# Copying strided operands for the value products, two more weight buffers from a dead table, and expert rows of 8 KB

## The reference

```
first_block, two layers:   h += 0.5 * swiglu(rmsnorm(h))
                           h += mixer(rmsnorm(h))        layer 0: ab_mixer, layer 1: c_mixer
                           h += 0.5 * swiglu(rmsnorm(h))
                           h += sigmoid(rmsnorm(h) @ Wg) * (p @ Wp)
second_block:              recurrence, pooling and attention branches, gated, merged into h
                           h += expert_choice_ffn(rms_norm(h))
                           out = rms_norm(h)

ab_mixer:  qa, ka, va, qb, kb, vb = split(xn @ w_in)
           banded attention on (qa, ka, va); on (qb, kb, vb) three groups of heads
           with dilations 1, 4 and 16 (tokens of one residue class attend each other)
expert_choice_ffn:
           aff = softmax(h @ router)                     16 experts
           vals, idx = top_k(aff.T, 64)                  each expert takes 64 tokens
           xg  = h[idx]
           y   = (silu(xg @ w_gate) * (xg @ w_up)) @ w_down * vals
           out[idx] += y
```

## Time and profile before

| | |
|---|---|
| median of 3 runs | 3620.35 us (3615.5 to 3622.46) |
| the profiled execution | 3626.29 us, span 3624.9 us |
| TensorE, weight loads busy | 3329.7 us (92%), 2544.3 us (70%) |
| VectorE, ScalarE, GpSimd busy | 44%, 30%, 9% |
| value products of ab_mixer | about 509 to 577 us |
| experts, from the first gate product | about 3104 to 3625 us |
| DMA packets | 96660, 445.89 MB |

### The profile page before, as it was taken

How to read it: one execution, slowest core, us unless ns; L and a number is a source line. 1 busy time by engine, 2 the same in 40 slices (tenths; PEclk the granted TensorE clock), 3 DMA queues, 4 the chain that set the end, 5 groups by cost and what they waited for, 6 DMA issues and landing times.

```text
span 3624.9 us, 52383 instructions
## 1 busy us (share of the span) xinstructions
PE 3329.7 (92%) x22912; PEld 2544.3 (70%) x22912; DVE 1606.8 (44%) x2207; ACT 1086.9 (30%) x1684; POOL 320.7 (9%) x374
## 2 busy tenths in 40 slices
PE   8999999999999999999999999668768998978876
PEld 6888787888887888886788877457656886423323
DVE  4443546544336443327544337854475444101102
ACT  4222215432224222226422233444324324000001
POOL 1000111100000000001100002131141002000001
PEclk9999999999999999999999999889988999999998
DMA  3223320122223222332122223000020223699996
GB/s 132 95 89 98 124 82 13 47 93 93 91 94 106 99 93 88 110 117 82 59 97 101 84 91 106 29 32 5 4 78 18 88 102 124 264 409 409 409 410 255
DMA packets 96660, 445.89 MB, mean 123 GB/s; under 512 B 8496, under 2 KB 9648, under 8 KB 78768
## 3 DMA queue, kind: packets, MB, share of 16 engines
q1 hardware_dynamic: 96432, 442.53, 33.5%
HBM read 440.40 MB, written 2.10 MB: 122 GB/s over the span
## 4 chain that ended last, share of the span: by engine, by line
PE 81%; DMA 8%; DVE 7%; ACT 2%; issue 2%; POOL 0%; SPq 0%; DVEq 0%; POOLq 0%; ACTq 0%
PE bank L165 21%; PE bank L166 21%; PE bank L167 21%; PE bank L2182 4%; DMA xe<-in_exp_up 3%; PE bank L1584 3%; PE bank L769 2%; DMA xe<-in_exp_gate 2%; PE bank L736 2%; PE bank L1576 2%; PE bank L752 2%; DMA xe<-in_exp_down 2%; PE bank L2258 1%; PE bank L651 1%; DVE w_lo L471 1%
## 5 line engine op out<-in xcount | busy, mean ns | idle before, releaser
L471 DVE TENSOR_TENSOR w_lo<-slot,w_hi 128x2048 fp32r<-128x2048 f32 (+4 forms) x243 | 489.3, 2014 | 344.5 <-ACT w_hi L462 343.2
L165 PE MATMUL bank<-xa,w_hi 128*128 128x512 f32 x1368 | 546.0, 399 | 22.1 <-DVE xa L514 10.2
L166 PE MATMUL bank<-xa,w_hi 128*128 128x512 f32 x1368 | 534.0, 390 | 0.0
L167 PE MATMUL bank<-xa,w_lo 128*128 128x512 f32 x1368 | 534.0, 390 | 0.0
L462 ACT ACTIVATE w_hi<-slot 128x2048 fp32r<-128x2048 f32 (+4 forms) x243 | 405.8, 1670 | 384.9 <-PE bank L167 383.8
L165 PE MATMUL bank<-xb,w_hi 128*128 128x512 f32 x832 | 326.6, 393 | 9.0 <-DVE w_lo L471 9.0
L166 PE MATMUL bank<-xb,w_hi 128*128 128x512 f32 x832 | 324.7, 390 | 0.0
L167 PE MATMUL bank<-xb,w_lo 128*128 128x512 f32 x832 | 324.7, 390 | 0.0
L165 PEld LDWEIGHTS bank<-xa,w_hi 128*128 128x128 f32 x1368 | 257.8, 188 | 83.9 <-issue 11.1
L166 PEld LDWEIGHTS bank<-xa,w_hi 128*128 128x128 f32 x1368 | 258.0, 189 | 58.9 <-issue 6.5
L167 PEld LDWEIGHTS bank<-xa,w_lo 128*128 128x128 f32 x1368 | 257.8, 188 | 54.1
(11 more groups left out here) (410 smaller groups left out, 5193.1 us busy)
## 6 DMA issues: line engine op xcount, KB each, us to landing
slot<-in_w_gu SPq DMA_DIRECT2D x87, 1024.0 KB, 4.9
slot<-in_exp_gate SPq DMA_DIRECT2D x48, 1024.0 KB, 13.5
slot<-in_exp_up SPq DMA_DIRECT2D x48, 1024.0 KB, 14.1
slot<-in_exp_down SPq DMA_DIRECT2D x48, 1024.0 KB, 14.2
slot<-in_w_dn SPq DMA_DIRECT2D x64, 704.0 KB, 4.0
slot<-in_w_gate SPq DMA_DIRECT2D x24, 768.0 KB, 4.2
xe<-in_exp_gate SPq DMA_DIRECT2D x16, 1024.0 KB, 14.1
xe<-in_exp_up SPq DMA_DIRECT2D x16, 1024.0 KB, 14.1
```

The source lines that it names most:

```text
L165: e.matmul(out, w[0], x[0], start=(j == 0), stop=False)
L166: e.matmul(out, w[0], x[1], start=False, stop=False)
L167: return e.matmul(out, w[1], x[0], start=False, stop=(j == n - 1))
L471: dve.e.tensor_tensor(lo, slot(k, b), hi.bitcast(F32), ALU.subtract).then_inc(L.up("w_lo", b))
```

## The change

It has three parts. The values of groups 2 and 3 read copies `xc` of `xa`, in which the tokens of a class lie side by side. ScalarE copies the rounded parts (`act_classes`), GpSimd the rests (`pool_classes`), both after the last rotation; the copies lie over the buffers of the rotation and over `sq`. The eight expert blocks that a product needs are laid out on the host so that a partition's 2048 floats are one row of 8 KB; which numbers go to which partition stays the same. And the ring gets two buffers more, over the table `G`, from expert block 24 on, once the last product with `G` is done.

```diff
 def expert_block(w, e, j):
-    return w[e, j * 256:(j + 1) * 256, :].rearrange("(k p) c -> p k c", p=P)
+    return w[e, j]
...
+    sq_area = a.copy()
     k.sq, k.sqsum = [a.buf(512, "sq") for _ in range(2)], a.buf(512, "sqsum")
...
-    inner = a.copy()
+    inner, b = a.copy(), a.copy()
...
-    m.rT = a.buf(8, "rT")
+    m.rT = b.buf(8, "rT")
+    m.xc = [b.pair("xc") for _ in range(KT - 1)] + [sq_area.pair("xc")]
...
+    late = a.copy()
     m.G = a.buf(4096, "G", F32R).rearrange("p (i s) -> p i s", i=4)
...
+    k.slots += [late.buf(SLOT, "slot") for _ in range(2)]
...
-                                      4: ("h", "n10", 7), 5: ("h", "n10", 7), 6: ("turned_xe", 7), 7: ("turned_xe", 7)}
+                                      4: ("h", "n10", 7), 5: ("h", "n10", 7), 6: ("turned_xe", 7), 7: ("turned_xe", 7),
+                                      8: ("dispatched", 1, 7), 9: ("dispatched", 1, 7)}
...
+        if b == k.first["exp"] + 24:
+            slots = [8, 9] + slots
...
-def pe_values(k, st, g, b, width, x, sel):
+def pe_values(k, st, g, b, width, x, sel, ready=()):
...
         for j in range(KT):
+            for name in ready:
+                pe.wait_ge(*L.at(name, st, j))
             last = three(e, bank[:, 0:width], each(lambda p: sel(p, i), x[j]), at(w, j), j, KT)
...
+def act_classes(k):
+    act, e, L, m = k.act, k.act.e, k.led, k.ab
+    act.wait_ge(*L.at("roped", "ab", 19))
+    for j in range(KT):
+        e.activation(f4(m.xc[j][0]), cls(k.xa[j][0].bitcast(F32)), ACT.Copy).then_inc(L.up("class_hi", "ab", j))
+
+
+def pool_classes(k):
+    pool, e, L, m = k.pool, k.pool.e, k.led, k.ab
+    pool.wait_ge(*L.at("roped", "ab", 19))
+    for j in range(KT):
+        e.tensor_copy(f4(m.xc[j][1]), cls(k.xa[j][1].bitcast(F32))).then_inc(L.up("class_lo", "ab", j))
...
-        pe_values(k, "ab", g, b["ab_v"] + g, 256, k.xa, AB_SEL[g])
+        pe_values(k, "ab", g, b["ab_v"] + g, 256, *((k.xa, tok) if g < 2 else (m.xc, tok, ("class_hi", "class_lo"))))
...
         act_weight(k, b["ab_v"] + g + 1)
+        if g == 0:
+            act_classes(k)
...
+    pool_classes(k)
     pool_attention(k, "ab", m.att, ab_units(k))
...
     for name in ("exp_gate", "exp_up", "exp_down"):
-        a[name] = f[f"{name}_2"][0]
+        w = f[f"{name}_2"][0].reshape(16, 4, 2, P, 1024)
+        a[name] = np.ascontiguousarray(w.transpose(0, 1, 3, 2, 4)).reshape(16, 4, P, 2048)
```

More of the change, by code:

```diff
@@ L910, in ab_units @@
     return units
-def by_class(x, i):
-    return cls(x)[:, i, :]
-AB_SEL = [tok, tok, by_class, by_class]
+def act_classes(k):
[8 more added lines that the diff above has]
+        e.tensor_copy(f4(m.xc[j][1]), cls(k.xa[j][1].bitcast(F32))).then_inc(L.up("class_lo", "ab", j))
 def sp_ab(k):
```

## The result

| | median us | range of the runs | profiled execution, span |
|---|---|---|---|
| before | 3621.40 | 3615.50 to 3630.30 (4) | 3626.29, 3624.9 |
| changed | 3582.19 | 3577.32 to 3595.42 (4) | 3583.27, 3582.0 |
| changed, compared again on another chip | 3583.18 | 3578.27 to 3595.74 (6) | 3595.74, 3594.4 |

The ratio to before is 0.9895, with a 95% interval of 0.9862 to 0.9929; the second comparison gives 0.9884 (0.9861 to 0.9908). By the medians the change makes the kernel 39 us faster (26 to 50 by the interval). The forecast was 3587 in a range of 3579 to 3594.

A forecast was written before the change was run, and what follows sets the result against it. TensorE was taken to bound the long part, expert-weight transfers the experts' stage. Savings of 21.8 + 3.4 + 8.2 = 33.4 us from the median 3620.35 gave 3587 us, range 3579 to 3594.

The forecast's parts named there:

- What bounds each stage: Whole kernel: TensorE sets the pace in the values and the tail, expert-weight transfers from 3170.64 us to nearly the end.
- Part 1, the class copies: Attention values, groups 2 and 3: eight banks at 2.88 instead of 5.60 us save 21.8 us; copies cost nothing.
- the chain behind ScalarE's queue: After ScalarE's copies: emptying group 0's banks, then splitting the third value block; a split start up to about 527.5 is free.
- Part 2, two buffers: Experts, ahead of pair 1: block 24 is issued earlier, removing the dry stretch; 3.4 us saved, between 0 and about 4.
- Part 3, rows of 8 KB: Expert blocks 16 to 175: 0.051 us less on each of 160 blocks, 8.2 us saved (1.9 to 13.6).
- full help: Experts, sign to look for: steps of two blocks at 4.96 us if long rows help fully; 5.03 was forecast.
- the short rate of 8 KB rows holds: Experts, rival: 13.6 us instead of 8.2, and 1.7 more if the tail's slow clock goes; 3580 us, chance 0.15.
- they hardly help: Experts, rival: bytes set the ceiling, so long rows gain only 1.9 us; 3593 us, chance 0.2.
- The last 16 blocks: Experts' tail after block 175: no gain counted, because TensorE is the limit from there.
- the slower one: Experts, rival: full queues of 8 KB rows run at 348 GB/s, 3.01 us a block; 3677 us, chance 0.03.
- The copies were not late: Value group 2, rival: slow class-step copies make TensorE wait, 4.4 us lost at 3.5 us a GpSimd copy; 3591, chance 0.07.
- the slow clock: Tail, part at a granted clock of 0.50: losing or keeping it is worth 1.7 us either way.

The follow-up runs named there:

- more copies: Changed kernel with each class copy made three times on ScalarE and twice on GpSimd, each waiting for the one before; ratio 0.9908 to the kernel before.
- queries by class: Changed kernel with the rotation writing the dilated groups' queries in class order, so that score-product loads are contiguous; ratio 0.9888 to the kernel before.

## Why the prediction was right

- **What bounds each stage: right.** TensorE in the values, transfers in the experts, TensorE in the tail, though there the transfers end at nearly the same time.
- **Part 1, the class copies: right, 0.5 us small.** Forecast 21.8 us, measured 44.8 - 22.5 = 22.3. A contiguous load out of `xc` takes 188 ns, a little less than one out of `xa` in groups 0 and 1 (192). The copies cost nothing on the path, as argued: 1.06 us each on ScalarE, between my 0.7 and 1.4, and 10.8 us for all on GpSimd, within 9 to 14. The run with more copies shows what it costs when the cover is gone, and that the chain behind ScalarE's queue is the one that I named.
- **Part 2, two buffers: right.** Forecast 3.4 us, measured 3.3 alone, in D. The time of that kernel can't show it.
- **Part 3, rows of 8 KB: right in kind, small in size.** Forecast 0.051 us on a block and 8.2 us, measured 0.067 to 0.07 (D with the rows alone, and 2.56 to 2.49) and so 10.7 to 11.2 us for 160 blocks. Steps follow at 4.98 us, nearer to the 4.96 that I named for full help than to my 5.03. A cost by row, half of which goes, was right. The mis-sized term is that cost: I took 0.067 us for the 256 rows of a 4 KB block, as the difference between 409 and 420 GB/s. The three sizes give 0.146 for 256 rows (387 to 409 GB/s, 2.710 to 2.564 us), so half is 0.073. The 420 of a short window was no rate free of the rows' cost: by the line through the three sizes a block without it would take about 2.42 us, or 434 GB/s (an estimate). Short windows can lie above the long run with rows of 8 KB too: 427 GB/s between 3106 and 3112 us in the changed kernel. The rival that the short rate of 8 KB rows holds (13.6 us) was about as near as my forecast; the one that they hardly help (1.9 us) was far off.
- **The last 16 blocks: nearly right.** I took nothing for them. In the kernels with rows of 4 KB and the copies or the buffers alone, whose tails run at full clock, the last step does wait for DMA, by 0.7 us, and from the last up step to the end it is 77.0 us. With rows of 8 KB at full clock it is 76.0 (rows alone) and 76.1 (queries by class). So these blocks are worth about 0.9 us at full clock. In the profile of before the last step doesn't wait; there the half-clock stretch makes TensorE's last product 1.7 us longer (15.57 us up to the combination, against 13.88 with the rows alone), which covers the 0.7.
- **Sum.** 22.3 + 3.3 + 11.2 = 36.8 us by the stages, 33.4 forecast, and 39 by the medians (26 to 50 by the interval).
- **Rivals.** The time alone can't choose: the interval takes in all cases but the slower one, and 3582 is nearer to the 3580 of the rival with short rates than to my 3587. The stages choose. The copies were not late. Long rows brought 10.7 to 11.2 us and not 1.9. They were not 13.6 either, and the slow clock did not leave the tail of the profile. The slower case would need 388 GB/s and got 420. The Trainium skill ("DMA: Bandwidth & Descriptors", Why small descriptors are slow) gives a packet about 3 cycles beside its beats of 32 bytes, which makes an estimate of 1.1% for 8 KB rows. The runs show 2.6% (2.564 to 2.497 us at 409 and 420 GB/s), so these cycles are not the whole cost of a row in this kernel, and the measurement decides.

## What to carry to other kernels

Where TensorE is the limit, look at the mean time of its weight loads by form: one that takes 330 instead of 190 ns reads its operand with a step, and a copy by engines that wait anyway buys it back; but only where the load is not hidden behind its product, which the length of the repeating unit tells and the load's own time does not. Where transfers are the limit, count rows, not only bytes: joining two rows of 4 KB gave 2.6% of the rate in the long run here. And two buffers added to the ring were worth the dry stretch of the queue and nothing else here; look for a rate below the full one before you add one. A tail that two engines end together gives nothing back when one of them is relieved, and two profiles can be compared there only at the same granted clock.

## What the hardware showed

- A DMA row has a cost of its own: full queues run at 387, 409 and 420 GB/s with rows of 2, 4 and 8 KB. The estimate from these is some 9 ns a row on its engine.
- ScalarE reads with a step of 16 bytes at 1.06 us for 128x512, eight in a row, against 0.71 for the row that writes `xa`. What the step costs GpSimd isn't shown, as no trace has a contiguous copy of 128x512: in the kernel with more copies a strided one takes 1.14 us, and four contiguous ones of 128 columns (0.29) would take 1.16. Its first copy takes 3.26 us. VectorE's split of 2.28 us starts at the same time (512.65) and takes no longer than elsewhere, and the copy ends 1.0 us after it, as if it had waited for VectorE. No run tests that. GpSimd's first two copies in that kernel:

```profile
512.66 3.26 POOL L936 CAST xc<-xa 128x512 fp32r<-128x512 f32 x1 [2.21 <-DVE kb L677]
515.98 1.14 POOL L938 CAST xc<-xa 128x512 fp32r<-128x512 f32 x1
```

- TensorE's streamed operand costs more with a step too: 398 against 271 ns for a product of 128 columns, and 2.03 against 1.57 us for a row of 12 score products of which 8 have it.
- After a wait of 11.2 us TensorE ran at a granted clock of 0.50 for 2.9 us (the kernel with more copies).
- Two executions of one kernel differed by 12.5 us, in step with 24 us more at half clock. A difference of that size between two single profiles is no evidence; a stage's length at an equal clock is.
